# A hybrid decoder step on one core: the adaLN products with weight blocks as the stationary side

## What is computed

```python
mod = jax.nn.silu(c) @ P['w_ada'] + P['b_ada']            # (9, 1024) @ (1024, 6144)
sh1, sc1, g1, sh2, sc2, g2 = jnp.split(mod, 6, axis=-1)
h = _rmsnorm(x, P['norm_pre_mix']) * (1.0 + sc1) + sh1
proj = h @ P['w_in']                                      # 1024 x 2560
y_rwkv = ...                                              # RWKV-7 time mixing
y_swa = ...                                               # sliding-window attention with sinks
x = x + g1 * _rmsnorm(concat(y_rwkv, y_swa) @ P['w_out'], P['norm_post_mix'])
h2 = _rmsnorm(x, P['norm_pre_ffn']) * (1.0 + sc2) + sh2
x = x + g2 * _rmsnorm(conv_ffn(h2), P['norm_post_ffn'])
```

## Time and profile before

| | us |
|---|---|
| median of 3 runs | 2037.49 |
| lowest and highest run | 2018.91, 2039.33 |
| span of the profiled execution | 2031.4 |
| PE busy | 1792.0 (88%) |
| PEld busy | 1638.3 (81%) |
| DVE busy | 928.1 (46%) |
| ACT busy | 603.9 (30%) |
| POOL busy | 178.5 (9%) |

### The profile page before, as it was taken

How to read it: one execution, slowest core, us unless ns; L and a number is a source line. 1 busy time by engine, 2 the same in 40 slices (tenths; PEclk the granted TensorE clock), 3 DMA queues, 4 the chain that set the end, 5 groups by cost and what they waited for, 6 DMA issues and landing times.

```text
span 2031.4 us, 28835 instructions
## 1 busy us (share of the span) xinstructions
PE 1792.0 (88%) x12280; PEld 1638.3 (81%) x12280; DVE 928.1 (46%) x1100; ACT 603.9 (30%) x837; POOL 178.5 (9%) x102
## 2 busy tenths in 40 slices
PE   6899996798798898988987947999999999999983
PEld 1899983355697887877967937999999999999983
DVE  3401028742534444444744057544554455445535
ACT  3311112344333342332342243232223222322222
POOL 0000008900100000000011222000000000000004
PEclk8899997898798898997998988999999999999987
DMA  8211112231000000000012031111011111111122
GB/s 304 73 43 51 42 63 69 83 122 42 1 1 2 1 1 2 1 1 28 1 66 105 22 125 48 50 45 52 31 49 54 45 38 41 62 41 41 41 102 84
DMA packets 29466, 105.17 MB, mean 52 GB/s; under 512 B 4472, under 2 KB 7304, under 8 KB 28224
## 3 DMA queue, kind: packets, MB, share of 16 engines
q1 hardware_dynamic: 29248, 103.02, 14.7%
q10 hardware_dynamic: 144, 1.06, 0.2%
HBM read 93.71 MB, written 11.40 MB: 52 GB/s over the span
## 4 chain that ended last, share of the span: by engine, by line
PE 77%; DVE 15%; ACT 4%; issue 2%; DMA 1%; DVEq 0%; POOL 0%; ACTq 0%; SPq 0%
PE ps L458 39%; PE ps L691 10%; PE ps L899 10%; PE ps L703 4%; PE ps L439 4%; PE ps L605 1%; DVE Z L1789 1%; PE ps L548 1%; PE ps L520 1%; DMA raw<-ada 1%; PE ps L622 1%; DVE nm L1472 1%; PE ps L678 1%; ACT UNI L1100 1%; DVE acc L1823 1%
## 5 line engine op out<-in xcount | busy, mean ns | idle before, releaser
L458 PE MATMUL ps<-XS,spl 128*128 128x344 f32 x5184 | 824.3, 321 | 38.2 <-DVE XS L1752 20.6
L458 PEld LDWEIGHTS ps<-XS,spl 128*128 128x128 f32 x5184 | 819.9, 189 | 41.6 <-issue 25.2
L899 PE MATMUL ps<-act,spl 128*128 128x344 f32 x1584 | 255.9, 322 | 9.8 <-DVE act L1801 9.0
L899 PEld LDWEIGHTS ps<-act,spl 128*128 128x128 f32 x1584 | 251.7, 190 | 12.6 <-issue 9.3
L1789 DVE SCALAR_TENSOR_TENSOR Z<-U,par,Z 128x1023 f32<-128x1023 f32 x88 | 112.9, 1283 | 162.0 <-ACT Z L1251 156.4
L1823 DVE TENSOR_TENSOR acc<-acc,ps 128x1032 f32<-128x1032 f32 x88 | 108.2, 1230 | 128.7 <-PE ps L899 128.6
L1233 ACT ACTIVATE spl<-raw 128x1024 fp32r<-128x1024 f32 x66 | 68.5, 1055 | 284.1 <-PE ps L899 198.4
L1416 DVE TENSOR_TENSOR spl<-raw,spl 128x1024 fp32r<-128x1024 f32 x28 | 34.2, 1225 | 233.1 <-ACT spl L970 233.0
L439 PE MATMUL ps<-raw,cTs 128*9 128x512 f32 x192 | 99.8, 673 | 36.5 <-DVE mod L1399 21.1
L1742 DVE TENSOR_TENSOR spl<-raw,spl 128x1024 fp32r<-128x1024 f32 x66 | 79.7, 1222 | 61.3 <-ACT spl L1233 60.1
L439 PEld LDWEIGHTS ps<-raw,cTs 128*9 128x9 f32 x192 | 17.4, 99 | 104.6 <-issue 70.3
(11 more groups left out here) (275 smaller groups left out, 2139.1 us busy)
## 6 DMA issues: line engine op xcount, KB each, us to landing
raw<-ada SPq DMA_DIRECT2D x48, 512.0 KB, 3.9
raw<-up SPq DMA_DIRECT2D x44, 512.0 KB, 3.4
raw<-down SPq DMA_DIRECT2D x22, 512.0 KB, 3.7
raw<-w_in SPq DMA_DIRECT2D x20, 512.0 KB, 3.4
xT<-xT SPq DMA_DIRECT2D x4, 1032.0 KB, 12.5
X<-xT SPq DMA_DIRECT2D x1, 4128.0 KB, 13.0
x_dram<-X SPq DMA_DIRECT2D x8, 516.0 KB, 2.6
X<-x_dram SPq DMA_DIRECT2D x1, 4128.0 KB, 12.7
```

The source lines that it names most:

```text
L458: mm = nc.tensor.matmul(ps[:, 3 * bank_set + t, 0:SL], w[:, a, k * P:(k + 1) * P], x[:, k, b, t * SL:(t + 1) * SL], start=(k == order[0] a ...
L899: mm = nc.tensor.matmul(ps[:, 3 * (down_set(i, y)) + t, 0:SL], w[:, a, k * P:(k + 1) * P], act2[:, f, b, t * SL:(t + 1) * SL], start=(f == ...
```

## The change

`ada_tile` now takes a tile that holds all 1024 rows for 128 output columns. It makes eight matmuls of it, each with a 128 x 128 block of weights as the stationary side and the nine conditions (128 x 9) as the moving one. The result is feature-major at once, 128 partitions x 9, and goes straight to the tile's place in PSUM: bank 0 in the first stage, bank 7 in the attention stage. The host lays out `w_ada` as it does the other weights. `ada_row`, the ACT copies (`ada_out`, 12 of them), the transposes (`ada_turn`, 48 of them) and their semaphores go. DVE's `modulation` waits for `ada_used` in place of `ada_turned`. The DMAs keep their number, size and order; `modulation` and the wait for `mod_added` keep their places.

```diff
-            def ada_tile(n, bank, loads):
+            def ada_tile(n, bank, at, loads):
 
                 pe.wait_ge(raw_in[n % 4], loads * 16)
-                for x in range(2):
-                    k = n % 4 * 2 + x
-                    mm = nc.tensor.matmul(ps[0:9, bank, :], cTs[:, k, :], raw[:, n % 4, x * 512:(x + 1) * 512],
+                for k in range(KD):
+                    mm = nc.tensor.matmul(ps[:, bank, at:at + 9], raw[:, n % 4, k * P:(k + 1) * P], cTs[:, k, :],
                                           start=(k == 0), stop=(k == KD - 1))
                 mm.then_inc(ada_used, 1)
-
-            def ada_turn(g, bank, at):
-
-                pe.wait_ge(s("ada_row"), g + 1)
-                for i in range(4):
-                    mm = nc.tensor.transpose(ps[:, bank, at + i * 9:at + i * 9 + 9], ada_row[:, i * P:(i + 1) * P],
-                                             ident[0:9, 0:9])
-                mm.then_inc(s("ada_turned"), 1)
...
-                    ada_tile(4 * g + x, 6 + g % 2, g + 1)
+                    ada_tile(4 * g + x, 0, (4 * g + x) * 9, g + 1)
...
-                if g >= 1:
-                    ada_turn(g - 1, 0, (g - 1) * 36)
-            ada_turn(ADA_A // 4 - 1, 0, ADA_A * 9 - 36)
...
-                g = (ADA_A + 2 * u) // 4
-                if u % 2 == 0 and u >= 2:
-                    ada_turn(g - 1, 7, 0)
                 turn_probs(u)
                 if u % 2 == 0 and u >= 2:
-                    pe.wait_ge(s("mod_added"), g - ADA_A // 4)
+                    pe.wait_ge(s("mod_added"), u // 2)
                 for n in (2 * u, 2 * u + 1):
-                    ada_tile(n, 7, (ADA_A + PC) // 4 + n // 4 + 1)
+                    ada_tile(n, 7, n % 4 * 9, (ADA_A + PC) // 4 + n // 4 + 1)
                 values(u)
-            ada_turn((ADA_A + ADA_B) // 4 - 1, 7, 0)
...
-            def ada_out(g, bank):
-                act.wait_ge(ada_used, 4 * (g + 1))
-                if g >= 1:
-                    act.wait_ge(s("ada_turned"), g)
-                nc.scalar.activation(ada_row[:], ps[0:9, bank, :], ACT.Copy).then_inc(s("ada_row"), 1)
-
...
-                if u >= 2 and u % 2 == 0:
-                    ada_out(ADA_A // 4 + u // 2 - 1, 7)
             move(2 * NT - 1)
-            ada_out((ADA_A + ADA_B) // 4 - 1, 7)
...
-                dve.wait_ge(s("ada_turned"), (first + count) // 4)
+                dve.wait_ge(ada_used, first + count)
...
-    a["ada"] = np.ascontiguousarray(v["w_ada"][0].reshape(4, 2, P, 12, 512).transpose(3, 0, 2, 1, 4)).reshape(48, P, D)
+    a["ada"] = _tiles(v["w_ada"][0])
```

More of the change, by code:

```diff
@@ L113, in build_program @@
         (rs,), _ = place([("rs", [P, N], F32)], TMP)
-        (ada_row,), _ = place([("ada_row", [9, 512], F32)], TMP + 8 * N)
         (rope, S4, PR, VA, Kf, Vf, KTs, kvrow, sS, sP, sPT, mx, nm, sk, den, rd), at = place([
@@ L963, in _ @@
             act.wait_ge(zeros_set, 1)
-            ada_out(0, 6)
             act.wait_ge(sumsq_ready, 1)
             inverse_root(slices(rs[:]), three(1), eps[:, 0:1], 1.0 / D).then_inc(std_ready, 1)
-            for g in range(1, ADA_A // 4):
-                ada_out(g, 6 + g % 2)
             def whi(slot2, slot4):
```

## The result

The kernel after takes 2074.81 us (median of 4 runs, 2071.47 to 2076.64). The ratio to the kernel before is 1.0209, with a 95% interval from 1.0158 to 1.026: slower, by 1.6 to 2.6%. The median of all four runs of before is 2036.95 us, so the medians differ by about 38 us. The forecast was 2024.5 and a range of 2005 to 2041. The profiled execution has a span of 2071.3 us, 39.9 more than before.

A forecast was written before the change was run, and what follows sets the result against it. It took the attention chain as mostly DVE-bound while POOL runs, with PE's tiles on it in even units, and PE-bound afterwards. Terms -3.1 + 0 - 5.5 - 4.4 = -13.0 took 2037.5 to 2024.5 us, range 2005 to 2041.

The forecast's parts named there:

- The price of a record: Condition tiles on PE: 0.062 us a record at 2.4 GHz, 0.110 at 1.2; two tiles 2.0 and 3.5 us.
- The mechanism of the clock: PE: loads do not raise the clock, with idle time they lower it; dense work behind then pays 2.2 us a fall.
- First stage: Tiles up to modulation: modulation starts at 49.3 rather than 52.47, -3.1 us.
- Attention with POOL: Attention units while POOL runs: 9.5 for 9.57 in even units, odd units gain nothing; 0 us.
- -5.5: Attention after POOL: odd units -6.1, even units +0.1, plus 0.5 allowed for cold tiles.
- -4.4: Last two attention units: row copy and turn gone, cheaper tiles, unit 14's saving limited by ACT.
- -1.6 and -0.5: Last two units: -1.6 us for the row copy and turn before unit 14's transposes, -0.5 for the last ada_out.
- Rival 2: A full-array load costs 0.107 to 0.117 us at 2.4 GHz too, warm tiles gain nothing: 2037 to 2041 us; chance 0.14.
- Rival 3: The clock never comes up in the attention stage: about +47, 2084 us; chance 0.08.
- rival 1: Loads count as activity and the clock stays up: together -31, 2006.5 us; chance 0.12.
- the term for the even units with POOL: Four even attention units while POOL runs, with the clock up: 7.8 for 9.57 us each, given as -6.

The follow-up runs named there:

- fourteen copies: Kernel after, with the nine conditions streamed fourteen times over (126 columns in place of 9), loads untouched: 2035.57 us, ratio 0.9993 to before.
- short tiles: Kernel after, with every second block of rows left out, four matmuls a tile in place of eight: 2018.3 us, ratio 0.9902 to before.

## Why the prediction was wrong

**The price of a record was wrong by a factor of two; this is the step that failed.** "I take 0.062, near L447" should have been 0.108 at 2.4 GHz (3.48 / 32) and "0.110 a record" should have been 0.216 at 1.2 GHz (13.82 / 64). Two tiles take 3.5 and 6.9 us, not 2.0 and 3.5. I misread two rows. L447 is a transpose of nine rows, one record to an instruction, and its records stand 0.06 to 0.07 apart; I named that difference and then chose it all the same. Whether transposing or the nine rows make it fast, no run separates; between 64 and 128 rows the traces show no difference (0.213 and 0.216 at 1.2 GHz). L583 alternates between two row groups, so its 0.11 was half of a load's time. The row that was nearest in every respect, L691 (float32 matmul, 128 rows, 128 columns loaded, 0.117), was in the bounds, and I set it aside because its stream is wide. The fourteen copies show that load and stream of about 128 columns are almost equally long there (0.108 and 0.112). No bound at all stood for the low clock above 0.110.

The Trainium skill's rule of columns divided by 1.2 (TensorE: Matmul & The Clock Gate, LDWEIGHTS) gives 107 ns for 128 columns, and no clock stands in it. Its number met the measured 0.108 at 2.4 GHz; at 1.2 GHz the traces show 0.216, and for L447's transposes 0.06 to 0.07 at 2.4 GHz, so the measurement decides: the time follows the granted clock, and it is not the same for L447's transposes as for a float32 matmul.

**The mechanism of the clock was right, its size was not.** The forecast said that the loads would not raise the clock, that with the idle time before them they would lower it, and that values and scores would then pay. All three are in the trace. But a tile pair twice as long is a stretch of almost no stream twice as long: here 3.5 us of it lowered the clock with no gap in front, so it falls in odd units too, where the forecast had it stay up. (Of 495.0 to 503.5 the forecast said that half of its records are L583; it is 32 of 46.) With short tiles the forecast comes out within 6 us (2018.3 against 2024.5), and with wide streams the long tiles cost nothing (2035.57). Long loads lose nothing where the stream beside them is wide, and narrow tiles half as long lose 1.6 us in an even unit; the 38 us need both.

**Point by point.** First stage: -3.1 forecast, +14.9 measured; the sum at the low clock was right (3.4 against 3.36), the tiles were not (7.0 and 14.1 against 13.82 and 24.28), and 1.2 of the rest is the later start that varies between traces. Attention with POOL: 0 forecast; from 327.58 the tiles of unit 6 at 423.02 start 95.4 later, against 88.2 for the same tiles before (312.58 to 400.82), so +7.2. From there to the tanh it is 108.5 against 90.25: +18.2, where the forecast had -5.5 and -4.4. The row copy and turn at the end did go. In the fourteen copies, whose tiles cost what the old ones did, it is 29.2 us from the last even tiles with a wait to the tanh (460.56 to 489.80) against 31.25 before (459.82 to 491.07): -2.0, where the forecast had -1.6 and -0.5 for them.

**Rivals.** Rival 2 had the right price at 2.4 GHz, and therefore the odd tiles right, but kept the cold tiles at 3.5 and the number of falls: 2037 to 2041. Rival 3 had the clock down throughout, 2084. The truth is rival 2's price with a clock between the two, and the range left it out because each rival changed one thing while price and clock depend on each other. In rival 1 the term for the even units with POOL was added wrongly: four times 9.57 - 7.83 is 7.0, not 6; nothing else hangs on it.

## What to carry to other kernels

Before turning a product round so that the large operand is the stationary one, price the load from a row of the same kind (type, rows, and matmul or transpose), and check whether neighbouring records use different row groups. A product with a narrow moving side can lower TensorE's clock although PE shows no gap, and the dense work behind it pays; while the load is the longer of the two, streaming copies costs next to nothing (0.112 us a record for 0.108 here), and here it brought back most of the clock. And ask of every wait what stands ahead of the instruction that ends it on its own engine: here one small addition, moved ahead of a mask, gained 27 us where the change was forecast to gain 13.

## What was not expected of the hardware

- The load of 128 float32 columns for a matmul: 0.108 us at 2.4 GHz and 0.216 at 1.2; for a transpose of nine rows (L447) four in 0.41 us with the last one's 0.20.
- Sixteen-record tiles with 9, 63 and 126 columns of stream: 2074.8, 2060.0 and 2035.6 us, with PE busy for 89, 89 and 88% of the span.
- Loads into the upper and the lower 64 rows ran side by side at 0.11 a record at 1.2 GHz, and 0.20 to 0.21 once only one group was left.
- The view of stretches gives a granted clock of 1.00 for 25.8 to 39.6 in after, although its records stand 0.216 apart; the first change of clock on record comes later, near the end of the sum of squares. Ahead of it that column says nothing in this trace; the distance between records does (65 in 13.80 us, then 29 in 3.00 and 21 in 4.00):

```profile
25.80:39.60 13.80, 13.80 (x65) 13.80 (x65) 2.56 (x3) 1.06 (x1) 0.00 (x0) 1.00 0.51 181
...
43.00:46.00 3.00, 3.00 (x29) 3.00 (x29) 0.00 (x0) 2.90 (x3) 0.00 (x0) 1.00 0.11 14
46.00:50.00 4.00, 4.00 (x21) 4.00 (x21) 2.11 (x2) 1.84 (x2) 0.00 (x0) 0.50 0.74 252
```
